# Reordering the mixer stage of a two-model transformer kernel: attention heads one gate slot earlier, side products in mid-slot, recurrence ahead of two remainders, Tanh gates

## What is computed

```python
c_q, c_kv, k_r, u_pool, z, xbc, dt, lru_g, lru_x, gates = jnp.split(u, pts, axis=-1)
y_a = mla_mixer(...)    # 8 heads: softmax(q k^T) v
y_b = pool_mixer(...)
y_c = ssd_mixer(...)    # y = (C B^T * exp(segsum(a))) (x dt) + x d_skip, times silu(z), rmsnorm
y_d = rglru_mixer(...)  # r_t, i_t sigmoids, a_t = exp(-8 r_t softplus(-lam)),
                        # u = xc * i_t * sqrt(1 - a_t^2), h = scan(a_t, u), times gelu gate
gates = jax.nn.sigmoid(gates.reshape(b, s, N_BRANCH, D_MODEL))
merged = (gates[:, :, 0] * (y_a @ w_branch[l, 0]) + gates[:, :, 1] * (y_b @ w_branch[l, 1])
        + gates[:, :, 2] * (y_c @ w_branch[l, 2]) + gates[:, :, 3] * (y_d @ w_branch[l, 3]))
x = x + merged @ w_out[l]
```

## Time and profile before

| | us |
|---|---|
| median of 3 runs | 1431.64 |
| lowest, highest | 1428.36, 1434.75 |
| the profiled execution | 1433.73, its span 1431.9 |

### The profile page before, as it was taken

The page is one execution under the profiler, slowest core; times in us unless marked ns, Lnnn a source line. Parts: engine busy times, 40 slices in busy tenths (PEclk is TensorE's granted clock), DMA queues, the critical chain, the costliest instruction groups (busy, mean ns, idle before and its releaser), DMA issues.

```text
span 1431.9 us, 18389 instructions
## 1 busy us (share of the span) xinstructions
PE 1357.3 (95%) x7504; PEld 745.7 (52%) x7504; DVE 923.1 (64%) x1132; ACT 705.8 (49%) x714; POOL 99.4 (7%) x56
## 2 busy tenths in 40 slices
PE   6999997798999989999999999999989989999996
PEld 4685553245654445555667545444445545454443
DVE  6686754677774486465567675574767767665575
ACT  5477665234553364354456344454534755354451
POOL 0000000000000022000033012000004000300000
PEclk9999998899999999999999999999999999999999
DMA  9375432544656655475610445676937306566682
GB/s 316 125 254 162 156 129 89 181 153 162 218 204 204 218 196 191 162 238 197 211 60 2 148 147 197 228 252 206 316 106 270 100 18 204 183 214 217 224 259 94
DMA packets 152653, 258.09 MB, mean 180 GB/s; under 512 B 8881, under 2 KB 81532, under 8 KB 152572
## 3 DMA queue, kind: packets, MB, share of 16 engines
q1 hardware_dynamic: 152572, 256.96, 53.5%
HBM read 255.87 MB, written 1.07 MB: 179 GB/s over the span
## 4 chain that ended last, share of the span: by engine, by line
PE 83%; DVE 7%; ACT 3%; issue 2%; DVEq 2%; DMA 1%; POOL 1%; SPq 0%; POOLq 0%; ACTq 0%
PE ps L1176 16%; PE ps L992 12%; PE ps L1226 10%; PE ps L711 10%; PE ps L694 7%; PE ps L994 6%; PE ps L1015 6%; DVE w_ring L1805 3%; PE ps L729 3%; PE ps L948 2%; ACT w_hi L1402 1%; PE ps L658 1%; PE ps L1112 1%; PE ps L1256 1%; PE ps L1213 1%
## 5 line engine op out<-in xcount | busy, mean ns | idle before, releaser
L1805 DVE SCALAR_TENSOR_TENSOR w_ring<-w_ring,w_hi 128x2048 f16<-128x2048 f32 (+2 forms) x206 | 460.9, 2251 | 191.6 <-ACT w_hi L1402 190.5
L1402 ACT ACTIVATE w_hi<-w_ring 128x2048 f16<-128x2048 f32 (+2 forms) x206 | 381.6, 1864 | 223.6 <-PE ps L1015 50.9
L992 PE MATMUL ps<-actT,w_hi 128*128 128x512 f16 x640 | 208.2, 379 | 1.1 <-issue 1.1
L994 PE MATMUL ps<-actT,w_ring 128*128 128x256 f16 x640 | 174.4, 273 | 0.0
L1176 PE MATMUL ps<-w_ring,arena 128*128 128x512 f16 x384 | 145.5, 379 | 0.0
L1402 ACT ACTIVATE arena<-ps 128x512 f16<-128x512 f32 (+6 forms) x87 | 60.5, 709 | 162.6 <-PE ps L994 77.2
L711 PE MATMUL ps<-w_hi,actT 128*128 128x512 f16 x448 | 137.1, 382 | 2.9 <-DVE w_ring L1805 2.9
L1176 PE MATMUL ps<-w_hi,arena 128*128 128x512 f16 x448 | 139.1, 379 | 0.0
L694 PE MATMUL ps<-w_hi,actT 128*128 128x512 f16 (+2 forms) x384 | 111.9, 371 | 2.9 <-DVE actT L1810 2.9
L1226 PE MATMUL ps<-w_hi,arena 128*128 128x512 f16 x384 | 102.5, 379 | 6.8 <-DVE arena L2574 6.8
L992 PEld LDWEIGHTS ps<-actT,w_hi 128*128 128x128 f16 x640 | 62.6, 98 | 77.1 <-issue 1.6
(11 more groups left out here) (419 smaller groups left out, 1915.6 us busy)
## 6 DMA issues: line engine op xcount, KB each, us to landing
w_ring<-in_dil_w_in SPq DMA_DIRECT2D x36, 1024.0 KB, 5.2
w_ring<-in_w_ff SPq DMA_DIRECT2D x32, 1024.0 KB, 5.1
w_ring<-in_exp_w_gate SPq DMA_DIRECT2D x64, 512.0 KB, 4.0
w_ring<-in_exp_w_up SPq DMA_DIRECT2D x64, 512.0 KB, 5.1
w_ring<-in_exp_w_down SPq DMA_DIRECT2D x32, 1024.0 KB, 4.9
w_ring<-in_w_in SPq DMA_DIRECT2D x24, 1024.0 KB, 5.1
w_ring<-in_sb_w_in SPq DMA_DIRECT2D x12, 1024.0 KB, 5.4
w_ring<-in_w_branch SPq DMA_DIRECT2D x8, 1024.0 KB, 4.8
```

Source lines behind the costliest of these rows:

```text
L992: pe.matmul(ps[:, bank + c, :], w_h[:, k, cols], aT[:, kk, :], start=(kk == 0), stop=False, skip_group_check=True)
L994: ins = pe.matmul(ps[:, bank + c, 0:S], w_l[:, k, cols], aT[:, kk, 0:S], start=False, stop=(kk == KD - 1), skip_group_check=True)
L1402: return act.activation(dst, src, ACT.Copy, scale=scale)
L1805: dve.scalar_tensor_tensor(out=lo16(h)[:, 0:kn * c], in0=w_ring[:, h % RING, 0:kn * c], scalar=W_POW, in1=hi16(h)[:, 0:kn * c], op0=ALU.mu ...
```

## The change

1. **Heads.** `mla_step(s)` is the three-part step of before. Step 0 (score 0) goes to the middle of slot 0, step i + 1 follows slot i for i < 7, step 8 (out 6, turn 7) goes to the middle of slot 7, and step 9 (out 7) follows slot 7. None is left in the branch stage; the transposes of `o_mla` follow its first piece.
2. **Side products.** `lru_gate(0)`, `lru_gate(1)`, `ssd_y` and `ssd_turn` go to the middle (between b = 0 and b = 1) of slots 3, 4, 5 and 6, through a new argument `mid` of `gemm_tok`. The two `lru_gate` stand ahead of `ssd_y` now, the first of them ahead of `ssd_cumsum(1)`; the waits on banks 6-7 follow this order. ACT's and DVE's orders are written out anew.
3. **Recurrence.** `lru_scan` stands in DVE's queue ahead of `lo(40)`; `lo(41)`, `lo(42)` stand behind the reading of branch 0, `lo(43)`, `lo(44)` behind that of branch 1, `lo(45)` behind that of branch 2. The remainders of `ycT` are ahead of head step 8.
4. **Gates.** Sigmoid(x) is 0.5 + 0.5 Tanh(x/2). ACT computes Tanh; DVE's reading computes (gate + 1) * y, and the factor 0.5 / 2048 goes into the rounding of the merged sum (`MIX_POW`).

```diff
+MIX_POW = A_POW * 0.5 / SUM_POW
@@ gemm_tok
                     ins.then_inc(sig("w_used"), 1)
+                    if b == 0 and mid:
+                        mid()
@@ ssd_cumsum(1)
-                    pe.wait_ge(sig("dm"), 1)
+                    pe.wait_ge(sig("lru_r"), 1)
@@ lru_gate
-                if i == 0:
-                    pe.wait_ge(sig("dm"), 2)
-                else:
-                    pe.wait_ge(sig("ssd_y"), 1)
+                pe.wait_ge(sig("dm"), i + 1)
@@ ssd_y
-                pe.wait_ge(sig("lru_r"), 1)
+                pe.wait_ge(sig("lru_i"), 1)
@@ PE's order
-            extra = {0: [ssd_cb, ssd_cumcol], 1: [ssd_xs], 2: [lambda: ssd_cumsum(0)], 3: [lambda: ssd_cumsum(1)],
-                     4: [lambda: lru_gate(0)], 5: [ssd_y], 6: [lambda: lru_gate(1)], 7: [ssd_turn]}
+            mids = {0: first_gate_half, 3: lambda: lru_gate(0), 4: lambda: lru_gate(1), 5: ssd_y, 6: ssd_turn, 7: last_gate_half}
+            extra = {0: [ssd_cb, ssd_cumcol], 1: [ssd_xs], 2: [lambda: ssd_cumsum(0)], 3: [lambda: ssd_cumsum(1)]}
             for i in range(8):
                 evacuated(g)
-                gemm_tok(10 + i, (g % 2) * 2, 512)
+                gemm_tok(10 + i, (g % 2) * 2, 512, mid=mids.get(i))
                 g += 1
...
+                mla_step(i + 1 if i < 7 else MH + 1)
@@ branches
                 branch(i, yT, 0, 0)
                 if i < 3:
                     if i == 0:
-                        mla_turn(MH - 1)
-                    branch(i, yT, 0, 1)
-                    if i == 0:
-                        mla_out(MH - 1)
-                    branch(i, yT, 1, 0)
-                    if i == 0:
                         pe.wait_ge(sig("mla_o"), MH)
                         transposes(0, o_mla, KM, "mla_oT_pe", 4)
+                        pe.wait_ge(*EVAC[15])
+                    branch(i, yT, 0, 1)
+                    branch(i, yT, 1, 0)
@@ ACT
-                act.activation(gates[:, :, 512 * i:512 * i + 512], bank_pair(g, 512), ACT.Sigmoid, scale=1.0 / SUM_POW)\
+                act.activation(gates[:, :, 512 * i:512 * i + 512], bank_pair(g, 512), ACT.Tanh, scale=0.5 / SUM_POW)\
...
+            hi(24)
+            mla_exp(0)
             for i in range(8):
                 gate(i)
                 hi(25 + 2 * i)
-                mla_exp(i)
-                for f in extra.get(i, []):
-                    f()
-                hi(26 + 2 * i)
-            act.wait_ge(sig("ycT_pe"), KM)
-            act.wait_ge(sig("lru_in"), 1)
-            rounded(ycT, 6, KM, "ssd_norm", "ycT_hi")
+                if i < 7:
+                    mla_exp(i + 1)
+                if i == 1:
+                    xs_out()
+                elif i == 3:
+                    dm_exp(1)
+                elif i == 4:
+                    lru_decay()
+                elif i == 5:
+                    lru_root()
+                if i < 7:
+                    hi(26 + 2 * i)
+                if i == 2:
+                    lru_sigmoid(0)
+                    dm_exp(0)
+                elif i == 3:
+                    lru_sigmoid(1)
+                elif i == 5:
+                    act.wait_ge(sig("ycT_pe"), KM)
+                    act.wait_ge(sig("lru_in"), 1)
+                    rounded(ycT, 6, KM, "ssd_norm", "ycT_hi")
             act.wait_ge(sig("mla_oT_pe"), KM)
             rounded(yaT, 4, KM, None, "yaT_hi")
+            hi(40)
+            act.wait_ge(sig("lru_out"), 1)
+            act.activation(ydT[:, :, 0:S], lru_g, ACT.Copy, scale=A_POW).then_inc(sig("ydT_hi"), 1)
             hi(41)
             hi(42)
@@ DVE
+            mla_step(0)
+            lo(24)
+            lru_conv((0, 1))
+            mla_step(1)
+            cb_mask()
+            lo(25)
+            lo(26)
+            mla_step(2)
+            lo(27)
+            ssd_xdt()
+            lru_conv((2, 3)).then_inc(sig("xcT"), 1)
+            lo(28)
+            ssd_skip()
+            mla_step(3)
+            lo(29)
+            decay(0)
+            lo(30)
+            mla_step(4)
+            decay_cb(0)
+            lo(31)
+            decay(1)
+            lo(32)
+            decay_cb(1)
+            mla_step(5)
+            lo(33)
+            lru_input()
+            lo(34)
+            ssd_out()
+            mla_step(6)
+            ssd_scale()
+            lo(35)
+            lo(36)
+            mla_step(7)
+            lo(37)
+            remainders(ycT, 6, KM, "ssd_norm", "ycT_hi", "ycT")
+            mla_step(8)
+            lo(38)
+            mla_step(9)
+            lo(39)
+            remainders(yaT, 4, KM, None, "yaT_hi", "yaT")
+            lru_scan()
             lo(40)
-            remainders(ycT, 6, KM, "ssd_norm", "ycT_hi", "ycT")
-            mla_o(MH - 1)
-            remainders(yaT, 4, KM, None, "yaT_hi", "yaT")
-            lo(41)
-            lo(42)
-            lru_scan()
...
-                    ins = dve.scalar_tensor_tensor(out=gt if i else x_norm[:, t, :], in0=y, scalar=1.0 / SUM_POW, in1=gt,
-                                                   op0=ALU.mult, op1=ALU.mult)
+                    ins = dve.scalar_tensor_tensor(out=gt if i else x_norm[:, t, :], in0=gt, scalar=1.0, in1=y,
+                                                   op0=ALU.add, op1=ALU.mult)
...
-                if i < 2:
-                    for h in ((43, 44), (45,))[i]:
+                if i < 3:
+                    for h in ((41, 42), (43, 44), (45,))[i]:
                         lo(h)
```

More of the change, by code:

```diff
@@ L681, in tile_ready, with gemm_tok @@
                 return lambda t, b: pe.wait_ge(sig("xp_dve"), 4 * i + 2 * t + b + 1)
-            def gemm_tok(n, bank, cols, turn=None):
+            def gemm_tok(n, bank, cols, turn=None, mid=None):
                 for b in range(2):
@@ L920, in ssd_turn, with mla_step, first_gate_half, last_gate_half @@
             def ssd_turn():
-                pe.wait_ge(sig("lru_i"), 1)
                 pe.wait_ge(sig("ssd_normed"), 1)
                 transposes(0, y_ssd, KM, "ycT_pe", 6)
-            extra = {0: [ssd_cb, ssd_cumcol], 1: [ssd_xs], 2: [lambda: ssd_cumsum(0)], 3: [lambda: ssd_cumsum(1)],
-                     4: [lambda: lru_gate(0)], 5: [ssd_y], 6: [lambda: lru_gate(1)], 7: [ssd_turn]}
+            def mla_step(s):
+                if 0 <= s - 2 < MH:
+                    mla_out(s - 2)
+                if s < MH:
+                    mla_score(s)
+                if 0 <= s - 1 < MH:
+                    mla_turn(s - 1)
+            def first_gate_half():
+                mla_step(0)
+            def last_gate_half():
+                mla_step(MH)
+            mids = {0: first_gate_half, 3: lambda: lru_gate(0), 4: lambda: lru_gate(1), 5: ssd_y, 6: ssd_turn, 7: last_gate_half}
+            extra = {0: [ssd_cb, ssd_cumcol], 1: [ssd_xs], 2: [lambda: ssd_cumsum(0)], 3: [lambda: ssd_cumsum(1)]}
             for i in range(8):
                 evacuated(g)
-                gemm_tok(10 + i, (g % 2) * 2, 512)
+                gemm_tok(10 + i, (g % 2) * 2, 512, mid=mids.get(i))
                 g += 1
[L931 to L936, removed]
+                mla_step(i + 1 if i < 7 else MH + 1)
+                for f in extra.get(i, []):
                     f()
-            mla_out(MH - 2)
             def branch(i, yT, b, t):
@@ L1508, in _ @@
             hi(23)
-            hi(24)
             def gate(i):
@@ L1838, in tile_low @@
                     else:
-                        ins = dve.scalar_tensor_tensor(out=rows[:, :, lo], in0=src, scalar=A_POW, in1=rows[:, :, hi],
+                        ins = dve.scalar_tensor_tensor(out=rows[:, :, lo], in0=src, scalar=MIX_POW, in1=rows[:, :, hi],
                                                        op0=ALU.mult, op1=ALU.subtract)
@@ L2086, in decay, with decay_cb @@
                 ins.then_inc(sig("dm"), 1)
[L2088 to L2093, removed]
+            def decay_cb(half):
+                dve.wait_ge(sig("dm_exp"), half + 1)
+                for j in range(4):
+                    ins = dve.tensor_tensor(dm[:, 4 * half + j, :], dm[:, 4 * half + j, :], cbm[:, half, :], ALU.mult)
+                if half:
+                    ins.then_inc(sig("dm_cb"), 1)
             def ssd_skip():
@@ L2115, in lru_input @@
             def lru_input():
[L2117 to L2123, removed]
                 dve.wait_ge(sig("lru_i"), 1)
                 dve.tensor_tensor(lru_i, lru_i, xcT, ALU.mult).then_inc(sig("lru_in"), 1)
+                dve.wait_ge(sig("lru_at"), 1)
+                dve.tensor_tensor(lru_r, lru_a, lru_a, ALU.mult)
+                dve.drain()
+                dve.scalar_tensor_tensor(out=lru_t, in0=lru_r, scalar=1.0, in1=lru_t, op0=ALU.add, op1=ALU.mult)\
+                    .then_inc(sig("lru_sq"), 1)
             def lru_scan():
@@ L2135, in lru_scan, with mla_step @@
                 dve.tensor_tensor(lru_g, lru_g, lru_r, ALU.mult).then_inc(sig("lru_out"), 1)
```

(21 more changed lines are left out.)

10 lines of the change are left out of this document (3 added, 7 removed).

## The result

| | before | changed |
|---|---|---|
| median us | 1430.07 (4 runs) | 1407.91 (4 runs) |
| lowest, highest | 1428.36, 1434.75 | 1406.17, 1408.52 |
| the profiled execution, its span | 1433.73, 1431.9 | 1408.41, 1406.5 |

The ratio is 0.983, with a 95% interval of 0.981 to 0.985. The forecast was 1407.

A forecast was written before the change was run, and what follows sets the result against it. PE was taken to wait on DVE's and ACT's order. The turn of tile 0 comes 26.2 us earlier; less 0.5 for clock and 0.7 for small waits, 25 us: 1431.6 to 1406.6, rounded 1407, range 1399 to 1420.

The forecast's parts named there:

- Where PE waits and why: Six PE waits of 1.34 to 6.81 us, up to 295.13 us, come from the order on DVE and ACT, not load.
- Gate stage, 116.6 us: Gate stage with all heads: 114.5 us of PE work plus three stalls gives 116.3, taken as 116.6 us.
- the third: Turn 7 in mid-slot 7 waits for DVE's scaling of head 6, a stall of about 0.5 us.
- Branch stage: From branch 0 to the turn of tile 0: 42.0 us, no wait at branch 2, one 2.1 us wait before the turn.
- Tanh at nothing: Tanh gates remove 12 of 19 ACT table loads, 15 us of ACT, costed at nothing for the kernel's time.
- Clock: Half-speed PE work after the new 2.1 us wait before the turn: 0.5 us lost, bounds 0 and 1.3.
- floor of PE's work: PE's own work in both stages without any stall, 114.5 and 43.2 us; 30.6 us gained, 1401.
- The total: Gain of 25 us over the whole kernel, 1431.6 to 1406.6 us, rounded 1407; forecast case's chance 0.62.
- Small waits: Rival: four mid-slot or turn waits are each followed by half-speed work, about 8 us more, 1415; chance 0.14.
- Half the gain: Rival: the heads' waits vanish but DVE is late at branch 2, so the reading waits stay, 1419; chance 0.14.
- No effect: Rival: the waits only move behind 295 us, to ACT's and DVE's chain for tile 0, 1430; chance 0.05.
- Slower: Rival: DVE's side work delays every head's turn, eight steps at 4.3 us, 34 us against 26 gained, 1440; chance 0.05.

The follow-up runs named there:

- e4: The kernel before with only the recurrence's new order on DVE and nothing else of the change; 1420.40 us, ratio to before 0.991.
- e1: The changed kernel with the recurrence put back behind lo(42), and lo(41), lo(42) ahead of the reading of branch 0; 1420.56 us, ratio to before 0.991.
- e3: The changed kernel with the heads one step later again on all three engines, as before; 1412.54 us, ratio to before 0.987.
- e8: The changed kernel with lo(45) behind branch 3's tile 0, decay(1) ahead of decay_cb(0), ssd_skip and ycT remainders behind head steps 3 and 8; 1403.79 us.
- e2: The changed kernel with the gates computed by Sigmoid again, with the factors of before; 1407.82 us, ratio to before 0.9825.
- e9: The changed kernel itself measured and profiled a second time, in a later session; 1407.04 us, against 1429.25 for the kernel before.
- e11: The changed kernel with three small idle-tile multiplications on DVE ahead of each head step 2 to 8, 1.1 us per step; 1409.60 us.
- e7: The changed kernel with eight small idle-tile multiplications on DVE ahead of each head step 2 to 8, 3.0 us per step; 1426.08 us.

## Why the prediction was right

- *Where PE waits and why (DVE's and ACT's order, not their load).* Right: e4 takes away the waits for the readings and leaves those of the heads, e1 brings the first back without the second, and both only reorder instructions. For the heads' waits, e3 shows part of the cause; how the rest divides is not shown.
- *Gate stage, 116.6 us.* Measured 116.60, of which PE's own work 114.73 (114.5 worked out) and waits 0.29, 0.92 and 0.66 (0.4, 0.6 to 0.9, 0.5). The size of the third was right by a wrong cause (e8). That the total agrees to the last digit is luck: the terms gave 116.0 to 116.3, and 116.6 was taken without a reason for the difference.
- *Branch stage.* Recurrence done at T + 11.4 (11.8), reading of branch 0 at T + 16.1 (16.6), no wait at branch 2, reading of branch 2 from T + 32.2 (32.2), turn at T + 41.9 (42.0) after a wait of 2.0 (2.1). The rounded durations are 0.5 us too long up to the reading of branch 0, and the order is right throughout. The data of half 43 with x behind it cost nothing.
- *Tanh at nothing.* 0.5 us between G and T, not visible in the medians (e2).
- *Clock.* The term that was mis-sized: 0.5 us with an upper bound of 1.3 taken; measured 1.7 in the profile of the changed kernel, 0 in that of e9. Its bound came from one wait of 2.27 us in the earlier trace rows with no fall behind it, a sample of one (the row has three instructions at full speed, not the eight that the prediction names). The clock that the kernel before had lost is given back in full but for this last loss: 7.5 us between G and W in the first profile, 9.1 in e9. The prediction has it only inside its floor of PE's work, not as a term of its own.
- *The total.* 25 us were expected between G and the end, 24.6 came between G and W in the two profiles. The medians of a session are only 22.2 apart, since the profiled execution of before was 3.7 us above the median of its runs. The forecast started from a median of 1431.6; from the 1430.07 that the result has, the same 25 us would give 1405. So the time of 1407 came closer than the gain did (25 for 22.2), and that is luck. In which stretch executions of before differ by that much stays open.
- *Rivals.* Small waits did not lower the clock of the gate stage (1.00, with waits of 0.3 to 0.9 us). By the Trainium skill ("TensorE: Matmul & The Clock Gate", "A second HAM failure mode: psum-queue depth-cycling") many short idles can; the trace shows no such swing at 0.3 to 0.9 us nor in e11 (waits of 0.7 to 1.5 us in the gate stage, still 1.00). In e7 the clock did swing, but behind single waits of 1.5 us and more, 17 us and more apart, so no run here shows the rule at work. Half the gain did not happen, and e3 shows how near it is: with the heads late, DVE's chain behind the recurrence is full. "No effect" fails by what lies behind W, which takes as long as before. "Slower" is bounded by e7.

## What to carry to other kernels

Where an engine with a third of its time idle makes another wait, look at what stands in its queue ahead of the item waited for, and put a long piece that nobody needs soon (here the recurrence, 5 us) where the next consumer has slack, not where it happens to be ready. Work out the new order by start times, from measured durations, engine by engine, down to the last consumer: a delay that all intermediate slacks hide comes out at the one place without slack (5.7 of 6.8 us in e3). Count the clock with the waits: here it was 7.5 of the 24.6 us. The slack of a producer is its own idle time just ahead of the item, step by step; it gave the price of a lag within 0.3 us (e11) and 1 us (e7, clock aside).

## What the runs showed of the hardware

The waits of PE between G and W, over all profiles here, held against the granted clock of the work behind them:

- Below 1 us none was followed by half-speed work (clock 0.50).
- From 1.3 to 2.6 us there are fifteen, and four were: 1.48 and 1.69 us in e7 (mean clock 0.88 over the next 14 us, both times some 1.7 us lost), and the 2.0 us ahead of the turn in the first profile of the changed kernel and in e2. The other eleven were not: 1.34 and 2.27 us before, 1.38 in e1, 2.28 and 2.03 in e4, 2.54 and 2.02 in e7, 2.02 in e9, 1.39, 1.50 and 2.01 in e11.
- From 2.8 us on all eleven were, in the kernel before (2.82 to 6.81 us), e1, e3, e4 and e7.

The wait ahead of the turn is nearly the same, 2.01 to 2.03 us, in six profiles, and cost 1.7 us of clock in two of them and nothing in four. So in the middle range the length of the wait alone does not say whether a loss follows. What decides was not found out, and a term of 0 or 1.7 us is to be kept open for each such wait.
